# Gate and up weights with eight consecutive rows per partition, and expert rows turned with a step of eight columns

## The reference, cut to what matters

```python
gate = jnp.sum(jax.nn.one_hot(expert_id, N_EXPERTS) * p_exp[..., None], axis=1)   # top 2 of 16 experts
y = jnp.zeros_like(x)
for e in range(N_EXPERTS):
    g, u = jnp.split(x @ w_gate_up[e], 2, axis=-1)      # w_gate_up[e]: 1024 x 512
    y = y + gate[:, e:e + 1] * ((jax.nn.silu(g) * u) @ w_down[e])   # w_down[e]: 256 x 1024
```

## Time and profile before

| | |
|---|---|
| median of 3 runs | 1824.66 us (1822.75 to 1825.25) |
| profiled execution, time | 1823.54 us |
| profiled execution, span from first to last instruction | 1821.7 us |
| mean granted TensorE clock | 0.949 |
| TensorE busy, share of the span | 88% |
| DMA packets, MB | 137801, 203.42 |

### The profile page before, as it was taken

The page is one execution under the profiler, slowest core; times in us unless marked ns, Lnnn a source line. Parts: engine busy times, 40 slices in busy tenths (PEclk is TensorE's granted clock), DMA queues, the critical chain, the costliest instruction groups (busy, mean ns, idle before and its releaser), DMA issues.

```text
span 1821.7 us, 24795 instructions
## 1 busy us (share of the span) xinstructions
PE 1603.1 (88%) x9879; PEld 1406.6 (77%) x9886; DVE 832.3 (46%) x1555; ACT 538.1 (30%) x1056; POOL 442.1 (24%) x482
## 2 busy tenths in 40 slices
PE   5979899999998999798999999999993599999920
PEld 5944599999997687678989898899992477777710
DVE  4048399999901454332246455544263011211117
ACT  4246222111113544341164655211111211011025
POOL 2700198422331000002333343231202100000045
PEclk8989999999999999999999999999997699999965
DMA  5100111223325500363311111235005577877545
GB/s 173 33 7 1 53 36 59 65 81 95 99 74 163 166 19 6 114 210 124 89 41 38 47 32 44 74 116 200 27 1 225 207 256 224 260 246 242 190 134 195
DMA packets 137801, 203.42 MB, mean 112 GB/s; under 512 B 14868, under 2 KB 89108, under 8 KB 137696
## 3 DMA queue, kind: packets, MB, share of 16 engines
q1 hardware_dynamic: 132512, 183.09, 31.6%
q0 software_dynamic: 5184, 18.88, 3.0%
HBM read 148.61 MB, written 53.33 MB: 111 GB/s over the span
## 4 chain that ended last, share of the span: by engine, by line
PE 81%; DVE 6%; POOL 4%; DMA 3%; ACT 3%; issue 2%; POOLq 0%; SPq 0%; DVEq 0%; ACTq 0%
PE psum L499 15%; PE psum L501 15%; PE psum L500 15%; PE psum L1221 9%; PE psum L1242 6%; PE psum L1078 3%; PE psum L1066 3%; PE psum L1040 2%; PE psum L944 2%; PE psum L1087 2%; PE psum L1138 1%; PE psum L1213 1%; DVE scores L1700 1%; POOL gathered_expert_out L895 1%; POOL y L900 1%
## 5 line engine op out<-in xcount | busy, mean ns | idle before, releaser
L499 PE MATMUL psum<-x_hi,ring_hi 128*128 128x384 f32 x768 | 259.0, 337 | 0.5 <-ACT v L1378 0.5
L501 PE MATMUL psum<-x_lo,ring_hi 128*128 128x384 f32 x768 | 256.6, 334 | 0.0
L500 PE MATMUL psum<-x_hi,ring_lo 128*128 128x384 f32 x768 | 256.5, 334 | 0.0
L834 POOL CAST ring_hi<-ring_raw 128x512 fp32r<-128x512 f32 x88 | 65.8, 748 | 565.8 <-PE psum L501 390.7
L1221 PEld LDWEIGHTS psum<-expert_rows_T,w_gate_up 128*128 128x128 f32 x1024 | 169.7, 192 | 8.5 <-issue 8.5
L499 PE MATMUL psum<-w_hi,x_hi 128*128 128x256 f32 x576 | 168.5, 293 | 5.0 <-DVE channel_vectors L1645 3.7
L1221 PE MATMUL psum<-expert_rows_T,w_gate_up 128*128 128x192 f32 x1024 | 171.6, 329 | 0.7 <-ACT expert_rows_T L1570 0.7
L500 PE MATMUL psum<-w_hi,x_lo 128*128 128x256 f32 x576 | 164.1, 285 | 0.0
L501 PE MATMUL psum<-w_lo,x_hi 128*128 128x256 f32 x576 | 163.9, 285 | 0.0
L499 PEld LDWEIGHTS psum<-x_hi,ring_hi 128*128 128x128 f32 x768 | 144.2, 188 | 1.7 <-ACT v L1378 0.7
L500 PEld LDWEIGHTS psum<-x_hi,ring_lo 128*128 128x128 f32 x768 | 144.2, 188 | 1.1
(11 more groups left out here) (325 smaller groups left out, 3200.3 us busy)
## 6 DMA issues: line engine op xcount, KB each, us to landing
w_gate_up<-in_w_gate_up SPq DMA_DIRECT2D x16, 2048.0 KB, 8.9
ring_raw<-in_w_in SPq DMA_DIRECT2D x64, 256.0 KB, 3.4
w_down<-in_w_down SPq DMA_DIRECT2D x16, 1024.0 KB, 6.4
x_by_expert<-zeros SPq DMA_DIRECT2D x32, 384.0 KB, 5.2
expert_rows<-x_by_expert SPq DMA_DIRECT2D x16, 768.0 KB, 11.1
y_by_expert<-expert_out SPq DMA_DIRECT2D x16, 768.0 KB, 7.4
gate_sigmoid<-sigmoid_out SPq DMA_DIRECT2D x15, 576.0 KB, 3.2
w_raw<-in_w_in SPq DMA_DIRECT2D x16, 512.0 KB, 4.3
```

The source lines that it names most:

```text
L499: nc.tensor.matmul(out, ah, bh, start=first, stop=False)
L500: nc.tensor.matmul(out, al, bh, start=False, stop=False)
L501: return nc.tensor.matmul(out, ah, bl, start=False, stop=last)
L834: link(g.tensor_copy(RHI[:, p_ % 2, :, :], RRAW[:, p_ % 2, :, :]))
```

## The change

The HBM view of the gate and up weights is regrouped: partition `p` now holds rows 8p to 8p + 7 of the 1,024 rows, which follow each other in HBM, so a partition's share is one run of 16 KB in place of eight runs of 2 KB. To match, the transposes that make `expert_rows_T` no longer take 128 neighbouring columns of `expert_rows`; for block `k` they take columns k, 8 + k, 16 + k and so on, 128 floats that lie 32 bytes apart. The sums run over the same features in another order. The tiles, their sizes in SBUF, the number of instructions, the semaphores and the other transfers are the same. The same edit is made in the branch for experts with more rows.

```diff
-    WG_D = I["w_gate_up"].rearrange("e (k p) n -> e p k n", p=128)
+    WG_D = I["w_gate_up"].rearrange("e (p k) n -> e p k n", p=128)
...
                             last = tr(PS[:, 4 + q % 2, c:c + MR],
-                                      XG[:, par, h, 128 * (2 * q + k):128 * (2 * q + k) + 128], IDENT[0:MR, 0:MR])
+                                      XG[:, par, h, :].rearrange("s (p k) -> s k p", k=KB)[:, 2 * q + k, :], IDENT[0:MR, 0:MR])
...
                                 last = tr(PS[:, 4 + s, c:c + MR],
-                                          XG[:, 0, h, 128 * (2 * s + k):128 * (2 * s + k) + 128], IDENT[0:MR, 0:MR])
+                                          XG[:, 0, h, :].rearrange("s (p k) -> s k p", k=KB)[:, 2 * s + k, :], IDENT[0:MR, 0:MR])
```

## The result

The changed kernel takes 1829.1 us (median of 16 runs, 1825.42 to 1833.87) against 1824.82 us before (16 runs, 1822.75 to 1828.26). The ratio is 1.0023 with an interval of 1.0014 to 1.0031: 2.6 to 5.7 us slower, 4.3 us by the medians. The forecast was 1830 and slower.

What follows compares the result with a forecast made beforehand. TensorE was taken to bound the expert stage, 19.11 us per expert, with no DMA on the chain. Transfer 0, products 0 and turn 6.7 us on 1823.54 us gave 1830 us; range 1822 to 1849 us.

Steps and rivals of the forecast that it cites:

- The transfer's term: Gate and up weights' transfer per expert: an earlier landing gains nothing, with 18.8 us of slack; 0 us.
- the late transfers: Rival at the turn: TensorE waits for rows queued behind the weights in 14 rounds; 29 us, 1853 us; chance 0.04.
- faster copies by ScalarE: Rival in the turn: fewer packets speed up ScalarE's copies; at most 5 us faster, 1818.5 us; chance 0.06.
- The turn's mechanism: Transposes of each expert's rows: stepped loads outlast the 82 ns between transposes, lengthening TensorE's chain in 15 turns; 6.7 us.
- The pace: Time per stepped word in the transposes' loads: between TensorE's 0.84 and VectorE's 1.04 ns; 6.7 us.
- The working for 0.84 ns: Timeline of one turn at 0.84 ns a word: load 107 ns, turn 0.29 us longer, 4.4 us in 15 turns.
- The sign that I gave: Median load of the transposes: 140 ns means hidden, 189 to 215 the forecast, 280 or more ScalarE's pace.
- The sum: Whole kernel: transfer 0, products 0 and turn 6.7 us on the profiled 1823.54 us give 1830 us.
- The rows taken for the pace: Profile rows of 8 far words: VectorE 1.04 ns a word, no step penalty; ScalarE 6 ns longer, 1.57 ns a word.
- The rival at ScalarE's pace: Transposes' loads at 1.57 ns a word or somewhat more: 1845.5 us; chance 0.25 including anything beyond.
- The Trainium skill's rule: Transposes' loads: fewer than two hits per 16-byte SBUF line cost pace; at half pace 116 ns, about 5.7 us.
- The waits for ScalarE: TensorE's waits in the turn for ScalarE's copies: the same number as before.

Runs made afterwards that it cites:

- runs_only: Only the weights' view regrouped into runs of 16 KB, transposes on neighbouring columns as in the kernel before; ratio 0.9996 (0.9987 to 1.0005).
- beside_step8: Changed kernel with the first eight of each turn's sixteen transposes put between gate and up products; 1826.62 us, ratio to the kernel before 1.0008.

## Why the prediction was right

- **The transfer's term, 0.** Right: `runs_only` is 0.9996 (0.9987 to 1.0005), which leaves no room for the late transfers, nor for the 5 us that faster copies by ScalarE might have brought. That longer runs would land no later than 8.9 us was wrong (9.5), without consequence, since the slack was 18.8 and 6.8 us.
- **The turn's mechanism.** Right: the load outgrows the 82 ns between two transposes and TensorE's path grows at each turn. The pair with transposes between products shows that the step costs nothing where the load is covered, the pair with four banks that it is a price per transpose.
- **The pace.** This is the term that was mis-sized. I took the middle between 0.84 and 1.04 ns a word, 6.7 us. It was the lower of the two: with half of the loads behind products (`beside_step8`), the median load is 188 ns, 188 - 82 = 106 for 128 words, 0.83 ns a word. The working for 0.84 ns gave a second group at 1.20, a turn of 2.13 us and 4.4 us in all; the trace has 1.15 and 2.12 in one turn, 1.23 and 2.20 in the next, and 4.2 in all. Some of that fit is luck: for the turn of before the same working gives 7 x 0.082 + 0.29 + 0.49 + 0.11 + 4 x 0.082 = 1.79 us where the trace has 1.84, and the prediction set its worked turns against the 1.84. The sign that I gave, the median load, would have misled: from 206 ns one reads (206 - 82) / 128 = 0.97 ns a word. In a row of transposes a load lasts longer than 82 + 107 = 189 ns, probably because it also waits for what is ahead of it.
- **The sum.** 1830 against 1829.1 is closer than the term deserves, and that is luck: 6.7 was 2.4 too much against the measured 4.3, which is just under the forecast of 4.4 to 9, and the profiled execution on which I put it lay 1.3 us below the median of the runs.
- **The rows taken for the pace.** VectorE's 8 words without a price and ScalarE's 6 ns were both poor guides. TensorE's load has a pace of its own for stepped words: 0.46 ns for neighbours, 0.83 with 32 bytes, and the shortest loads with the other steps are 1 to 12 ns longer than with 32. The 0.83 is close to the 0.84 of the products' loads, which read neighbours; no run tells whether that has one cause. The rival at ScalarE's pace (+22 us) is refuted by every step.
- **The Trainium skill's rule** (Advanced Engine Details and Errata, Memory Cachelines): a price for the step of 32 bytes is there, and 106 ns is near the estimated 116 (with the 2 ns of the working, that estimate gives 6.1 us and not 5.7). But the rule makes the price hang on two hits in a 16-byte line, and the step of 8 bytes, with two words in each line, pays as much (217 ns). The measurement decides: for these loads it isn't the line.
- **The waits for ScalarE.** I expected as many as before. For the loads there are as many, 15, but shorter, 5.0 us in all against 7.0; the working lets the wait for group 0 shrink in this way.

## What to carry to other kernels

Before regrouping an HBM view for longer runs, see whether the transfer is on the chain at all; here 8 times longer runs could gain nothing, and their price was paid where the operand is read with a step. A stepped stationary operand cost here only what its load exceeds the stream ahead of it, so compare the two: behind a stream of 160 ns the step was free, behind 82 ns it cost 27 ns each time. And a stall for the copies out of PSUM both hid a part of that cost and was worth more than it: four banks in place of two gave 10 us by the medians (7.1 to 12.2).

## What the runs showed of the hardware that I had not expected

- Loads of the stationary operand for a float32 transpose run at about 0.46 ns a column over neighbours and 0.83 ns with a step of 32 bytes. Every step tried has about that price: the shortest load is 185 and 186 ns with 32 and 64 bytes, 194 to 197 with 8, 16 and 28.
- The 2 MB of weights landed 8.9 to 9.0 us after issue in runs of 2 KB (six kernels), 8.3 in runs of 4 KB and 8.4 in runs of 8 KB (one kernel each), and 9.4 to 9.6 in runs of 16 KB (four kernels). Longer isn't always sooner; why 16 KB is later was not tried.
- A transpose between two matmuls with their own loads costs more than in a row of transposes (115 against 82 ns), most likely because its short stream doesn't cover the load of the product behind it.
